# Gate and up projections of a gated MLP as seven block products instead of eight, down products one chunk behind

## The chip, the cores and the metric

One core of a Trainium2 chip runs the whole program. The metric is the device time of one execution in microseconds (us). The engines work in parallel, each through its own list of instructions in order: TensorE (PE in the profile) multiplies matrices, VectorE (DVE) and ScalarE (ACT) do elementwise work, GpSimd (POOL) does elementwise work too and issues some transfers, and SyncE (SP) issues the transfers of the weights. They wait for each other by semaphores.

## The reference

One inference step of a two-layer encoder on 640 token rows (512 of a prompt, 8 sequences of 16). What the change touches is the gated MLP that ends each layer:

```python
def conv_ffn(h, prev, w_gate, w_up, conv_w, conv_b, w_down):
    t = h.shape[1]
    g = h @ w_gate                                   # (tokens, 1024) @ (1024, 2816)
    gp = jnp.concatenate([prev.astype(g.dtype), g], axis=1)
    c = conv_b
    for j in range(CONV_W):                          # 3 taps over time
        c = c + conv_w[j] * gp[:, j:j + t]
    y = (jax.nn.gelu(c) * (h @ w_up)) @ w_down       # (tokens, 2816) @ (2816, 1024)
    return y, gp[:, t:]
...
    h = rmsnorm(x, p["ln_ffn"][l])
    f, tail = conv_ffn(h, conv_prev[l], ...)
    x = x + f
```

All is float32. The other parts of a layer (a mixer, cross-attention, their projections) are the same in both kernels.

## The kernel before

**Products in three parts.** Every float32 operand of the large products is split into a high part, rounded to the type TensorE takes, and a low part, the rest. One product of tiles is three matmuls into the same PSUM bank: weight-low by x-high, weight-high by x-low, high by high (`three`, L792, and the six matmuls of `cols_tile`, L858 to L863). For weights, ACT writes the high part (`w_hi`, L1563) and DVE the low part (`w_lo<-raw,w_hi`, L2093), in units of 128x1024 elements.

**Gate and up.** The 2816 features are 22 tiles of 128 (FT). A chunk ("gu", l, j) holds the weights of tiles 2j and 2j+1 of gate and up: 1024 rows by 512 columns, 4 units, so 11 chunks in each of 2 layers. Features lie on the partitions of the result and the 640 tokens along the free side. A bank holds 512 columns, so `cols_tile` runs each of the 4 outputs (gate and up, 2 tiles each) over 8 row blocks of the input in two pieces of 384 and 256 tokens: 8 x 3 x 2 matmuls, 192 in a chunk. ACT copies the gate out of PSUM to `gp`, applies the first tap (L1912), DVE the other two (L2520, L2521), ACT the gelu (L1919), DVE multiplies with the up result straight out of PSUM (L2524 to L2528), and ACT and DVE split the product `af` in `a_hi` (L1924) and `a_lo` (L2532).

**Down.** ("dn", l, g) multiplies a group of 4 tiles (the first group has 2) with the down weights, for 5 token tiles and 2 column halves, and DVE adds each bank to the residual stream `x` (L2146). Its place is after the chunks of the following group.

**Order and buffers.** Each engine's program is written out by hand as a list and runs in order. Weights are loaded by SP in pieces of two units to `raw`, which has 2 buffers; a load waits until the low parts of the load two places earlier are made. High and low parts lie in 5 slots (W_SLOTS). A slot is filled again when the matmuls of its unit are done. Results of large products rotate over 5 banks (`lin`): the product that takes a bank waits until the result five places earlier has been read out. POOL's part is small: after each squaring of a tile of `x` by ACT it makes the factor of the norm (`norm_rstd`, L538, L539), DVE then scales the tile (`xn<-x,rstd,gain`, L2115), TensorE transposes it (L820), ACT and DVE split the result in `hT_hi` and `hT_lo` (L1624, L2132). In the last projection before the MLP, ("co", l, 1), the norm of a tile runs beside the projection of the next, and the first gate and up products run beside the norm of the last two tiles (`norm_behind`).

## Time and profile before

| | us |
|---|---|
| median of 3 runs (lowest, highest) | 2069.16 (2069.08, 2069.41) |
| the profiled execution | 2069.33 |
| its span, first to last instruction | 2067.5 |
| TensorE busy | 2038.8 (99%) |
| VectorE busy | 981.7 (47%) |
| ScalarE busy | 763.9 (37%) |
| GpSimd busy | 198.6 (10%) |
| granted TensorE clock, mean | 0.997 |

A matmul's recorded duration holds a fixed latency beside its streaming, and consecutive matmuls overlap. What a matmul costs is the distance between its start and the next one's. DVE instructions overlap too, by less than 0.1 us.

The first MLP runs from about 603 us to 1070 us of the span, the second in the last part of the program.

### The profile page before, as it was taken

What the parts mean: (1) busy time and instruction counts of PE and PEld (TensorE: products, weight loads), DVE (VectorE), ACT (ScalarE), POOL (GpSimd) and SP (SyncE); (2) the same over time, 40 slices, a digit from 0 to 9 for tenths busy, and PEclk for the clock granted to TensorE, in tenths of its full rate; (3) what the DMA queues carried; (4) which work ended last, traced back from release to release, by engine and by line L of the source; (5) the groups of instructions that cost most, each with busy time, mean ns of one, the idle gap of its engine ahead of it and who ended that gap; (6) DMA issues with size and microseconds to landing.
All of it is one profiled execution on the core that took longest, in us unless ns stands there. A gap on an engine that the chain in (4) does not pass through costs nothing.

```text
span 2067.5 us, 30583 instructions
## 1 busy us (share of the span) xinstructions
PE 2038.8 (99%) x12398; PEld 1797.0 (87%) x12398; DVE 981.7 (47%) x1648; ACT 763.9 (37%) x1318; POOL 198.6 (10%) x458
## 2 busy tenths in 40 slices
PE   9999989999999999999999999999999999999997
PEld 7889767987789999999989888799778999999996
DVE  5453664435444443443453467653545444343443
ACT  4222552435344233232244447243534433223232
POOL 3012121000100000000010124210010000000001
PEclk9999999999999999999999999999999999999999
DMA  5324143245622122222221211723572222212221
GB/s 176 124 79 149 52 162 129 92 152 187 243 85 83 62 82 83 91 69 62 76 77 62 82 55 34 275 77 117 197 285 85 65 79 82 78 56 82 82 82 55
DMA packets 111066, 219.42 MB, mean 106 GB/s; under 512 B 7011, under 2 KB 52367, under 8 KB 110862
## 3 DMA queue, kind: packets, MB, share of 16 engines
q1 hardware_dynamic: 91234, 148.00, 21.4%
q0 software_dynamic: 19696, 69.47, 9.9%
q8 instruction: 102, 1.67, 0.3%
q14 instruction: 34, 0.28, 0.0%
HBM read 200.51 MB, written 18.24 MB: 106 GB/s over the span
## 4 chain that ended last, share of the span: by engine, by line
PE 95%; DVE 2%; ACT 2%; issue 1%; DMA 0%; POOL 0%; SPq 0%; DVEq 0%; ACTq 0%; POOLq 0%
PE bank L794 15%; PE bank L796 15%; PE bank L795 15%; PE bank L858 7%; PE bank L860 7%; PE bank L862 7%; PE bank L859 5%; PE bank L861 5%; PE bank L863 5%; PE bank L820 1%; PE bank L1240 1%; PE bank L1256 1%; PE bank L1197 1%; PE bank L1282 1%; PE bank L1293 1%
## 5 line engine op out<-in xcount | busy, mean ns | idle before, releaser
L2093 DVE TENSOR_TENSOR w_lo<-raw,w_hi 128x1024 fp32r<-128x1024 f32 x265 | 319.2, 1220 | 508.9 <-ACT w_hi L1563 505.0
L1563 ACT ACTIVATE w_hi<-raw 128x1024 fp32r<-128x1024 f32 x265 | 275.1, 1054 | 254.6 <-PE bank L796 203.5
L794 PE MATMUL bank<-w_hi,hT_lo 128*128 128x512 f32 x720 | 290.7, 404 | 3.1 <-DVE w_lo L2093 1.9
L858 PE MATMUL bank<-hT_hi,w_lo 128*128 128x384 f32 (+1 forms) x856 | 290.1, 339 | 0.0
L860 PE MATMUL bank<-hT_lo,w_hi 128*128 128x384 f32 (+1 forms) x856 | 289.3, 338 | 0.0
L862 PE MATMUL bank<-hT_hi,w_hi 128*128 128x384 f32 (+1 forms) x856 | 289.3, 338 | 0.0
L796 PE MATMUL bank<-w_hi,hT_hi 128*128 128x512 f32 x720 | 281.9, 391 | 0.0
L795 PE MATMUL bank<-w_lo,hT_hi 128*128 128x512 f32 x720 | 281.2, 391 | 0.0
L859 PE MATMUL bank<-hT_hi,w_lo 128*128 128x256 f32 (+1 forms) x856 | 239.0, 279 | 0.0
L861 PE MATMUL bank<-hT_lo,w_hi 128*128 128x256 f32 (+1 forms) x856 | 239.0, 279 | 0.0
L863 PE MATMUL bank<-hT_hi,w_hi 128*128 128x256 f32 (+1 forms) x856 | 239.0, 279 | 0.0
L2146 DVE TENSOR_TENSOR x<-x,bank 128x512 f32<-128x512 f32 x160 | 109.7, 686 | 155.1 <-PE bank L796 154.3
L794 PEld LDWEIGHTS bank<-w_hi,hT_lo 128*128 128x128 f32 x720 | 135.7, 188 | 42.6 <-issue 10.3
L794 PE MATMUL bank<-w_hi,a_lo 128*128 128x512 f32 x440 | 171.7, 390 | 0.0
L796 PE MATMUL bank<-w_hi,a_hi 128*128 128x512 f32 x440 | 171.3, 389 | 0.0
L795 PE MATMUL bank<-w_lo,a_hi 128*128 128x512 f32 x440 | 171.2, 389 | 0.0
L858 PEld LDWEIGHTS bank<-hT_hi,w_lo 128*128 128x128 f32 (+1 forms) x856 | 160.0, 187 | 1.5
L796 PEld LDWEIGHTS bank<-w_hi,hT_hi 128*128 128x128 f32 x720 | 135.5, 188 | 29.5
L859 PEld LDWEIGHTS bank<-hT_hi,w_lo 128*128 128x128 f32 (+1 forms) x856 | 160.1, 187 | 0.5
L862 PEld LDWEIGHTS bank<-hT_hi,w_hi 128*128 128x128 f32 (+1 forms) x856 | 160.0, 187 | 0.6
L860 PEld LDWEIGHTS bank<-hT_lo,w_hi 128*128 128x128 f32 (+1 forms) x856 | 160.0, 187 | 0.6
L861 PEld LDWEIGHTS bank<-hT_lo,w_hi 128*128 128x128 f32 (+1 forms) x856 | 160.1, 187 | 0.2
(372 smaller groups left out, 2997.4 us busy)
## 6 DMA issues: line engine op xcount, KB each, us to landing
raw<-w_ffn_gate SPq DMA_DIRECT2D x44, 512.0 KB, 4.1
raw<-w_ffn_up SPq DMA_DIRECT2D x44, 512.0 KB, 5.1
raw<-w_ffn_down SPq DMA_DIRECT2D x22, 1024.0 KB, 4.9
kcX<-cache_mem_k POOLq DMA_DIRECT2D x16, 1024.0 KB, 6.1
vcX<-cache_mem_v POOLq DMA_DIRECT2D x16, 1024.0 KB, 6.9
raw<-w_in_even SPq DMA_DIRECT2D x13, 1024.0 KB, 5.6
raw<-w_in_odd SPq DMA_DIRECT2D x12, 1024.0 KB, 5.2
raw<-w_cq SPq DMA_DIRECT2D x8, 1024.0 KB, 7.5
```

What stands on the lines that cost most here:

```text
L794: pe.matmul(out, wl, xh, start=first, stop=False)
L795: pe.matmul(out, wh, xl, start=False, stop=False)
L796: return pe.matmul(out, wh, xh, start=False, stop=last)
L858: pe.matmul(oa, wl, hT_hi[:, k, 0:HA], start=f, stop=False)
L859: pe.matmul(ob, wl, hT_hi[:, k, HA:TOK], start=f, stop=False)
L860: pe.matmul(oa, wh, hT_lo[:, k, 0:HA], start=False, stop=False)
L861: pe.matmul(ob, wh, hT_lo[:, k, HA:TOK], start=False, stop=False)
L862: ia = pe.matmul(oa, wh, hT_hi[:, k, 0:HA], start=False, stop=l)
L863: ib = pe.matmul(ob, wh, hT_hi[:, k, HA:TOK], start=False, stop=l)
L1563: act.activation(w_hi[:, g % W_SLOTS, 0:n], raw[:, q % 2, UNIT * i:UNIT * i + n], ACT.Copy).then_inc(*hi_made.mark(c, u))
L2093: dve.tensor_tensor(w_lo[:, s, 0:n], raw[:, q % 2, UNIT * i:UNIT * i + n], flat(w_hi[:, s, 0:n]), ALU.subtract).then_inc(*lo_made.mark(c, u))
L2146: ins = dve.tensor_tensor(xs, xs, lin.bank(c, t, *key)[:, :], ALU.add)
```

## The change

Gate and up become one product of 2x2 blocks: the 640 tokens are cut in two halves of 320, the 1024 input rows in two halves of 512, and the two feature tiles of a chunk are the two column blocks. A form of Strassen's identity makes the four result blocks with seven block products instead of eight. The weights of the products are the blocks A11, A12, A22 and the sums S1 to S4; their partners are the quarters of the transposed input or sums of them (t1, t2, t3, n4).

- The sums of the weights are made in each chunk by POOL, four of 128x1024 (`weight_sum`): S1 = A21+A22 to a buffer of its own, S3 = A11-A21, S2 = S1-A11, S4 = A12-S2 in place in `raw`. A gate-and-up chunk so has 7 units to split by ACT and DVE instead of 4.
- The sums of the input are made once for each layer, by DVE (t1, t2, each in two pieces) and POOL (t3, n4), from `hF`, a copy that ACT makes of the transposed input, and split by ACT and DVE.
- Each of the 7 units is multiplied for gate and for up: 4 row blocks x 3 matmuls of 320 tokens into one bank. A chunk has 14 such products, 168 matmuls.
- The result blocks are put together: ACT copies the first product to `p1` and the second to its place; POOL adds them (`first_corner`); DVE makes u2 = p1 + (S2 product), p1 = u2 + (S1 product), and from these the other three blocks (`to_sums`, `c22`, `c12`, `c21`). The up result is so in SBUF (`af`) when DVE multiplies it with the gelu (`gated`).
- The order of the MLP is a new list, FFN_PLAN: chunks 0 and 1, down group 0, then two chunks and a down group each, at the end chunks 8, 9, 10 and down groups 4 and 5. The taps of the second tile, the gelu, the multiplication and the splits of a chunk are issued among the instructions of the next chunk or down group.
- The first product of the first chunk follows the last projection tile directly; the transposes of the last two norm tiles stand behind the first and third product.

```diff
+FFN_PLAN = [("gu", 0), ("gu", 1), ("dn", 0)]
+for _g in range(1, GROUPS - 2):
+    FFN_PLAN += [("gu", 2 * _g), ("gu", 2 * _g + 1), ("dn", _g)]
+FFN_PLAN += [("gu", FT // 2 - 3), ("gu", FT // 2 - 2), ("gu", FT // 2 - 1), ("dn", GROUPS - 2), ("dn", GROUPS - 1)]
+PARTS = ("A11", "A12", "S1", "S2", "S3", "S4", "A22")
...
@@ sync: loads of the weights @@
-                    sp.wait_ge(*lo_made.at(oc, ou + on - 1))
+                    sp.wait_ge(*lo_made.at(oc, PARTS.index("A22" if ou else "S4") if oc[0] == "gu" else ou + on - 1))
...
@@ gpsimd @@
+                def weight_sum(j, part):
...
+                    pool.tensor_tensor(out, a, b, op).then_inc(*pool_done.mark("sum", l, j, part))
+                def first_corner(j, key):
+                    pool.wait_ge(*lin_a.at(("gu", l, j), (key, "A12")))
+                    dst = gp[0][:, HALO:HALO + HT] if key == "g" else af[0][:, 0:HT]
+                    pool.tensor_tensor(dst, dst, p1[key][:, :], ALU.add)...
...
@@ tensor @@
+                def gate_up(j, between={}):
+                    for u, part in enumerate(PARTS):
+                        wait_unit(c, u)
+                        if j == 0:
+                            wait_operand(part)
+                        hi, lo = operand[part]
+                        for m, key in enumerate("gu"):
+                            out = lin.open(pe, c, (key, part))
+                            for k in range(KT // 2):
+                                cols = slice(P * (2 * k + m), P * (2 * k + m) + P)
+                                ins = three(out[:, 0:HT], weight(c, u, False)[:, cols], weight(c, u, True)[:, cols], lo[:, k, :], hi[:, k, :],
+                                            k == 0, k == KT // 2 - 1)
+                            ins.then_inc(*lin_full.mark(c, (key, part)))
+                            if (part, key) in between:
+                                between[part, key]()
...
-                            cols_tile(c, f"ffn{l}", P * e, ("g", e))
-                            cols_tile(c, f"ffn{l}", 256 + P * e, ("u", e), last=e == 1)
+                        gate_up(i, {("A11", "g"): lambda: norm_tile(nm, T - 2), ("A12", "g"): lambda: norm_tile(nm, T - 1)} if i == 0 else {})
...
@@ vector @@
+                def to_sums(j, key):
+                    dve.wait_ge(*pool_done.at("C11", l, j, key))
+                    dve.wait_ge(*lin_full.at(c, (key, "S2")))
+                    dve.tensor_tensor(u2[key][:, :], p1[key][:, :], lin.bank(c, (key, "S2"))[:, 0:HT], ALU.add)...
+                    dve.tensor_tensor(p1[key][:, :], u2[key][:, :], lin.bank(c, (key, "S1"))[:, 0:HT], ALU.add)...
...
+                sum_t(0)
+                low_ts(0)
+                sum_t(1)
+                low_ts(1)
+                halves(nm, T - 1)
```

**The GpSimd list at the start of the MLP.** L538 and L539 (L592 and L593 in the new file) are the two instructions of a norm tile; `sum`, `sumN` and `raw` written by L763 are the weight sums. Before:

```order
L538 TENSOR_SCALAR rstd<-sq_sum 128x1
L539 TENSOR_TENSOR rstd<-rstd,half_neg 128x1
L538 TENSOR_SCALAR rstd<-sq_sum 128x1
L539 TENSOR_TENSOR rstd<-rstd,half_neg 128x1
L696 COPY gp_184<-prevT 128x8x2
L698 COPY tailc<-gp_184 128x2
```

and now:

```order
L592 TENSOR_SCALAR rstd<-sq_sum 128x1
L593 TENSOR_TENSOR rstd<-rstd,half_neg 128x1
L763 TENSOR_TENSOR raw<-sum_199,raw 128x8x128
L592 TENSOR_SCALAR rstd<-sq_sum 128x1
L593 TENSOR_TENSOR rstd<-rstd,half_neg 128x1
L763 TENSOR_TENSOR raw<-raw 128x8x128
L796 TENSOR_TENSOR t3F<-hF 128x1280
L798 TENSOR_TENSOR hF<-hF,t2F 128x4x320
L771 COPY gp_201<-prevT 128x8x2
L771 COPY gp_202<-prevT 128x8x2
L777 TENSOR_TENSOR gp_201<-gp_201,p1g 128x320
L777 TENSOR_TENSOR af_205<-af_205,p1u 128x320
```

A weight sum now follows directly on each norm tile from the second on, and two sums of the input follow the last.

**The VectorE list at the start of the first chunk.** `hF`, `t2F` and `t_lo` are the sums of the input. Before:

```order
L2093 TENSOR_TENSOR w_lo<-raw,w_hi 128x1024 x3
L2146 TENSOR_TENSOR x<-x,bank 128x512
L2115 SCALAR_TENSOR_TENSOR xn<-x,rstd,gain 128x1024
L2132 TENSOR_TENSOR hT_lo<-bank,hT_hi 128x4x128 x4
L2093 TENSOR_TENSOR w_lo<-raw,w_hi 128x1024
```

and now:

```order
L2409 TENSOR_TENSOR x<-x,bank 128x512
L2369 SCALAR_TENSOR_TENSOR xn<-x,rstd,gain 128x1024
L2389 TENSOR_TENSOR hT_lo<-bank,hT_hi 128x4x128
L2785 TENSOR_TENSOR hF<-hF 128x4x192
L2787 TENSOR_TENSOR t2F<-hF 128x4x192
L2791 TENSOR_TENSOR hT_lo<-hF,hT_hi 128x4x192
L2791 TENSOR_TENSOR t_lo<-t2F,t_hi 128x4x192
L2785 TENSOR_TENSOR hF<-hF 128x4x128
L2787 TENSOR_TENSOR t2F<-hF 128x4x128
L2791 TENSOR_TENSOR hT_lo<-hF,hT_hi 128x4x128
L2791 TENSOR_TENSOR t_lo<-t2F,t_hi 128x4x128
```

Eight instructions on the sums of the input stand behind the scaling of the last norm tile, before anything of the chunk.

**The VectorE list between two chunks.** From the last instruction on the banks of a chunk to the first on those of the next. Before, such an instruction stands in every tile (L2524 to L2528):

```order
L2093 TENSOR_TENSOR w_lo<-raw,w_hi 128x1024 x3
L2520 SCALAR_TENSOR_TENSOR cv_187<-gp_185,conv_par,cv_187 128x656
L2521 SCALAR_TENSOR_TENSOR cv_187<-gp_185,conv_par,cv_187 128x656
L2524 TENSOR_TENSOR af_189<-cv_187,bank 128x384
L2526 TENSOR_TENSOR af_189<-cv_187,bank 128x128
```

and now:

```order
L2840 TENSOR_TENSOR af_206<-u2u,bank 128x320
L2849 SCALAR_TENSOR_TENSOR cv_204<-gp_202,conv_par,cv_204 128x656
L2850 SCALAR_TENSOR_TENSOR cv_204<-gp_202,conv_par,cv_204 128x656
L2861 TENSOR_TENSOR af_205<-cv_203,af_205 128x512
L2864 TENSOR_TENSOR af_205<-cv_203,af_205 128x128
L2339 TENSOR_TENSOR w_lo<-raw,w_hi 128x1024
L2869 TENSOR_TENSOR a_lo<-af_205,a_hi 128x640
L2861 TENSOR_TENSOR af_206<-cv_204,af_206 128x512
L2864 TENSOR_TENSOR af_206<-cv_204,af_206 128x128
L2339 TENSOR_TENSOR w_lo<-raw,w_hi 128x1024
L2869 TENSOR_TENSOR a_lo<-af_206,a_hi 128x640
L2339 TENSOR_TENSOR w_lo<-raw,w_hi 128x1024
```

Eleven instructions with all their tensors in SBUF stand in a row, and the next bank is read only behind them.

## Rows read from the trace of the kernel before

**Rows 1.** The page: busy time, and the chain that ended last by engine.

```profile
PE 2038.8 (99%) x12398; PEld 1797.0 (87%) x12398; DVE 981.7 (47%) x1648; ACT 763.9 (37%) x1318; POOL 198.6 (10%) x458
...
PE 95%; DVE 2%; ACT 2%; issue 1%; DMA 0%; POOL 0%; SPq 0%; DVEq 0%; ACTq 0%; POOLq 0%
```

**Rows 2.** Waits of TensorE: us in total, times, longest.

```profile
PE bank L1016 <- DVE sA L2348: 3.2, 3, 2.4
...
PE bank L794 <- DVE hT_lo L2132: 0.7, 3, 0.3
```

**Rows 3.** Timeline of PE: start us, duration us, instruction, at the first MLP.

```profile
611.65 0.33 PE L794 MATMUL bank<-hT_hi,w_lo 128*128 128x384 f32 x1
...
613.56 0.33 PE L796 MATMUL bank<-hT_hi,w_hi 128*128 128x384 f32 x1
613.73 0.28 PE L794 MATMUL bank<-hT_hi,w_lo 128*128 128x256 f32 x1
...
619.36 0.28 PE L796 MATMUL bank<-hT_hi,w_hi 128*128 128x256 f32 x1
619.48 0.34 PE L858 MATMUL bank<-hT_hi,w_lo 128*128 128x384 f32 x1
...
626.52 0.34 PE L858 MATMUL bank<-hT_hi,w_lo 128*128 128x384 f32 x1
```

**Rows 4.** Groups of DVE by shape, whole run: count | busy us, mean ns.

```profile
L2093 DVE TENSOR_TENSOR w_lo<-raw,w_hi 128x1024 fp32r<-128x1024 f32 x264 | 318.9, 1224 | 504.8 <-ACT w_hi L1563 500.8
...
L2521 DVE SCALAR_TENSOR_TENSOR cv<-gp,conv_par,cv 128x656 f32<-128x656 f32 x44 | 39.7, 902 | 1.6
...
L2532 DVE TENSOR_TENSOR a_lo<-af,a_hi 128x640 fp32r<-128x640 f32 x44 | 36.3, 826 | 35.5 <-ACT a_hi L1924 35.5
L2524 DVE TENSOR_TENSOR af<-cv,bank 128x384 f32<-128x384 f32 x44 | 24.4, 555 | 44.7 <-PE bank L862 25.8 <-ACT cv L1919 18.9
```

**Rows 5.** Group of ACT by shape, whole run.

```profile
L1563 ACT ACTIVATE w_hi<-raw 128x1024 fp32r<-128x1024 f32 x264 | 274.8, 1057 | 254.6 <-PE bank L796 203.5 <-PE bank L863 42.3 <-DMA raw<-w_in_even 4.9
```

**Rows 6.** Timeline of POOL and DVE, two stretches where both work.

```profile
1242.94 3.24 DVE L2569 SCALAR_TENSOR_TENSOR of<-of,hs_rstd,gnorm 128x256 f32<-128x256 f32 x2 [0.81 <-POOL hs_rstd L717]
...
1243.61 0.41 POOL L729 TENSOR_TENSOR xL<-bcum 128x128 f32<-128x128 f32 x1
...
1245.79 0.89 POOL L735 TENSOR_TENSOR aI<-bcum 128x256 f32<-128x256 f32 x1
...
1274.79 1.11 POOL L753 TENSOR_TENSOR aS<-bcum 128x512 f32<-128x512 f32 x1
1274.93 2.43 DVE L2569 SCALAR_TENSOR_TENSOR of<-of,hs_rstd,gnorm 128x256 f32<-128x256 f32 x2 [0.81 <-POOL hs_rstd L717]
...
1275.84 1.24 POOL L755 TENSOR_TENSOR kdS<-bcum 128x512 f32<-128x512 f32 x1
```

**Rows 7.** DVE L2569 and L2588, 256 elements each: duration ns min/median/max.

```profile
L2569 DVE SCALAR_TENSOR_TENSOR of<-of,hs_rstd,gnorm x20: 477/546/2679, 1207.3 to 1320.3; 128x256 f32<-128x256 f32 x20
...
L2588 DVE SCALAR_TENSOR_TENSOR qI<-qI,cqT x8: 411/421/422, 1180.5 to 1269.7; 128x256 f32<-128x256 f32 x8
```

**Rows 8.** Timeline at the start of the first MLP, all engines.

```profile
608.04 0.55 POOL L539 TENSOR_TENSOR rstd<-rstd,half_neg 128x1 f32<-128x1 f32 x1
...
608.69 1.29 DVE L2115 SCALAR_TENSOR_TENSOR xn<-x,rstd,gain 128x1024 f32<-128x1024 f32 x1 [2.20 <-POOL rstd L539]
...
610.03 1.25 PE L820 MATMUL bank<-ident,xn 128*128 128x128 f32 x8
```

**Rows 9.** The clock: TensorE's timeline after its longest wait, and windows with PEclk.

```profile
269.12 0.66 PE L1016 MATMUL bank<-ident,sA 128*128 128x128 f32 x4 [2.35 <-DVE sA L2348]
...
270.00:275.00 5.00, 5.00 (x23) 4.20 (x23) 2.44 (x6) 1.55 (x3) 1.44 (x2) 0.66 0.99 360
```

**Rows 10.** The page: weight loads, KB each, median us from issue to landing.

```profile
raw<-w_ffn_gate SPq DMA_DIRECT2D x44, 512.0 KB, 4.1
raw<-w_ffn_up SPq DMA_DIRECT2D x44, 512.0 KB, 5.1
```

More of the change, by code:

```diff
@@ L123, in rest @@
         out += [("co", l, 0), ("co", l, 1)]
-        for g in range(GROUPS):
-            out += [("gu", l, j) for j in group_pairs(g)]
-            if g:
-                out.append(("dn", l, g - 1))
-        return out + [("dn", l, GROUPS - 1)]
+        return out + [(kind, l, i) for kind, i in FFN_PLAN]
     chunks += rest(0)
@@ L156 @@
 for _c in CHUNKS:
-    for _u in range(0, units_of(_c), 2):
-        _n = min(2, units_of(_c) - _u)
+    for _u in range(0, raw_units(_c), 2):
+        _n = min(2, raw_units(_c) - _u)
         for _i in range(_n):
@@ new lines, in rest @@
+                pool.wait_ge(*dve_done.at("t2F", l, 1))
+                pool.tensor_tensor(hF[:, 1, :, 0:HT], hF[:, 1, :, 0:HT], t2F[:, :, :], ALU.subtract).then_inc(*pool_done.mark("n4F", l))
+                pool.wait_ge(*act_done.at("prevT", l))
+                for j in range(FT // 2):
+                    more = j + 1 < FT // 2
+                    halo(2 * j)
+                    halo(2 * j + 1)
+                    first_corner(j, "g")
+                    first_corner(j, "u")
+                    if more:
+                        weight_sum(j + 1, "S1")
+                        weight_sum(j + 1, "S3")
+                    tails(2 * j)
+                    if more:
+                        weight_sum(j + 1, "S2")
+                    tails(2 * j + 1)
+                    if more:
+                        weight_sum(j + 1, "S4")
@@ L1309, in rest @@
                     ins.then_inc(*aux_full.mark("prevT", l, n))
[L1310 to L1311 removed]
+                nm = f"ffn{l}"
+                for t in range(T):
+                    if t:
+                        proj_out(("co", l, 1), t)
+                    else:
+                        out_steps(("co", l, 1), 0, 2, 8)
+                    if 0 < t < T - 1:
+                        norm_tile(nm, t - 1)
@@ L2472, in rest @@
                 add_x(("co", l, 0), TP, 0)
-                out_half(1, ("co", l, 1), f"cross{l}", f"ffn{l}")
+                nm = f"ffn{l}"
+                for t in range(T):
+                    if t == 1:
+                        split_lo(NEXT[("co", l, 1)], [0])
+                    if t == T - 1:
+                        split_lo(NEXT[("co", l, 1)], [1, 2, 3])
+                    add_x(("co", l, 1), t, 1, f"cross{l}")
+                    scaled(nm, t)
+                    if t:
+                        halves(nm, t - 1)
                 def down(g):
@@ L2535, in rest, with sum_t @@
-                down(GROUPS - 1)
+                def sum_t(n):
+                    for half in range(2):
+                        dve.wait_ge(*act_done.at("hF", l, T - 1 if n else T - 2, half))
+                    w, v = CUT[n], slice(HT + CUT[n].start, HT + CUT[n].stop)
+                    dve.tensor_tensor(hF[:, 0, :, w], hF[:, 0, :, v], hF[:, 0, :, w], ALU.subtract).then_inc(*dve_done.mark("t1F", l, n))
+                    dve.wait_ge(*dve_done.at("t1F", l, n))
+                    dve.tensor_tensor(t2F[:, :, w], hF[:, 1, :, v], hF[:, 0, :, w], ALU.subtract).then_inc(*dve_done.mark("t2F", l, n))
@@ new lines, in c21 @@
+                def c21(j, key):
+                    c = ("gu", l, j)
+                    dve.wait_ge(*lin_full.at(c, (key, "A22")))
+                    dve.wait_ge(*lin_v.at(c, (key, "S3")))
+                    dst = gp[1][:, HALO:HALO + HT] if key == "g" else af[1][:, 0:HT]
+                    dve.tensor_tensor(dst, u2[key][:, :], lin.bank(c, (key, "A22"))[:, 0:HT], ALU.add).then_inc(*lin_v.mark(c, (key, "A22")))
+                    if key == "g":
+                        dve_done.after("gate", l, 2 * j + 1)
```

443 lines of the change are left out of this document (348 added, 95 removed).

## The prediction

> **What bounds the kernel now.** I read the page first: TensorE is busy 99% of the span, the chain that ended last runs 95% through it, and no other engine is above 47% [rows 1]. Then TensorE's waits: its largest one was 2.4 us in a piece of attention, and on the norm's operands ahead of projections it waited 0.7 us in all [rows 2]. So the program is a row of matmuls, and in the MLPs it has no gap. What a matmul costs there I read from the distance of starts in its timeline [rows 3]: 12 matmuls of 384 columns begin from 611.65 to 613.56 us, 1.91/11 = 0.1736 us each; 48 of 256 columns from 613.73 to 619.36 us, 5.63/47 = 0.1198 us each; and one tile of `cols_tile`, 24 pairs, takes 626.52 - 619.48 = 7.04 us, 0.2933 us a pair, which is the sum of the two. Last I read the groups of VectorE and the stretches where GpSimd and VectorE both work, since the change loads these two.
>
> **What TensorE gains.** Removed are 22 chunks x 96 pairs = 2112 pairs: 2112 x 0.2933 = 619.5 us. Added are 22 x 168 = 3696 matmuls of 320 columns. The trace has none, but it has both neighbours; halfway between 0.1198 and 0.1736 is 0.1467 us, so 542.2 us. The ends are 0.1198 x 3696 = 443 us and 0.1736 x 3696 = 642 us; I take the midpoint, since the two rows lie on one line with the 7.04 us tile. Down products, transposes and the rest keep their number. The gain is 77.3 us. A product of 12 matmuls lasts 1.76 us, a weight unit 3.52 us, a chunk 24.64 us instead of 28.16 us.
>
> **What VectorE and GpSimd get.** For each chunk VectorE has 7 low parts, which start 1.15 us apart in a queue (1.22 us recorded, ends overlap) [rows 4]: 8.1 us. Reading out banks is twelve 320-column operations; between 0.42 us for 256 elements [rows 7] and 0.56 us for 384 [rows 4], less the overlap of 0.08 us, 0.40 us each: 4.9 us. Four taps of 0.9 us are 3.6 us, two multiplications of 640 elements 1.6 us, two low parts of `a` 1.5 us [rows 4]. Sum about 20 us in 24.64 us; before it was far below half. ScalarE gets three more high parts of 1.06 us [rows 5] and the copies, about 14 us, and is not the limit. GpSimd gets four sums of 1024 elements: 128 elements take 0.41 us and 512 take 1.11 us [rows 6], 1.8 ns an element, so 2.05 us each, and two `first_corner` of 0.76 us: 9.8 us.
>
> **The two do not run side by side.** In the stretch at 1242.9 us two VectorE instructions of 256 elements took 3.24 us together, the second 2.68 us, while GpSimd's row of subtractions ran; at 1274.9 us two took 2.43 us, each ending only after a GpSimd subtraction of 512 elements [rows 6]. Undisturbed such an instruction takes 0.42 us [rows 7]. All operands of these lie in SBUF. So a VectorE instruction with two SBUF inputs waits out a GpSimd instruction that reads SBUF, and GpSimd waits too (L735 took 0.89 us). I see no such stretch of a VectorE instruction that reads a bank. The Trainium skill, "SBUF — State Buffer", section "Who interferes with whom", says this as a rule against the change: the two share a read interface, and whoever issues first keeps it for the whole instruction. The trace agrees (2.68 us for 0.42 us of work).
> Of VectorE's 20 us in a chunk 14.8 us have two SBUF inputs (low parts, taps, multiplications), and GpSimd's 9.8 us all read SBUF. In a pair of chunks between two down groups the sums for the second chunk fall in the first one; those for the chunk after fall in the down group, where VectorE has room.
>
> **Start of an MLP.** Here the sum goes along the row of instructions. Before, the factor of the last norm tile ends at 608.6 us, VectorE scales at 608.69 us for 1.29 us, TensorE transposes at 610.03 us [rows 8]. Now a weight sum follows each factor on GpSimd without a wait, so it has the port when VectorE's scaling (two SBUF inputs) comes 0.1 us later: 2.05 us later for each of four tiles. VectorE has little room between these tiles, so it adds up: by my timeline the transposes of the third tile come 1.0 us late, the first block product 1.6 us, the transposes of the last tile 3.7 us (block products of 7 us stand ahead of S1, and only three of the four can hide it). Behind the last tile come copy, t1, t2, their splits back and forth between ScalarE and VectorE in two pieces, about 6.6 us from the scaled tile to the operand of S1, with 2.7 us of TensorE work left beside it: 3.9 us. Together 10.2 us. If GpSimd's t3 (1280 elements, 2.5 us) takes the port ahead of the second piece, 12.7 us. Without any blocking only the last chain is left, and one late tile: 4.4 us. I take 10.5 us a layer, ends 4.4 and 12.7.
>
> **Between chunks.** A product may take its bank when the one five places earlier has been read. The S1 product for gate waits for S2 (full 12.5 us after the chunk's start), VectorE reads both in 1 us, and the bank is wanted at 15.84 us: 2.3 us of room. In the first chunk of a pair nothing is left over from before, and VectorE keeps up until the loads land (issue after the low part of S4, then some 5 us [rows 10]). Then S1, S3, S2, S4 of the next chunk, 2.05 us each, stand one by one ahead of a low part or a tap. By my timeline VectorE is through with the first chunk's banks at 29.5 us, with taps, multiplications and splits at 41.4 us, and with the S2 and S1 products at 42.3 us, where the bank was wanted at 40.5 us: TensorE waits 1.9 us in the second chunk. Without blocking VectorE is there by 35 us, and the wait is nothing. The second chunk makes no sums, so the next pair starts clean. Chunks 8, 9, 10 have no down group between them: 1.9 us and then 5.6 us. Chunk 0 begins late and is followed by chunk 1: 4 us. So 3 x 1.9 + 1.9 + 5.6 + 4 = 17.2 us a layer at most by this reckoning, 0 at least. Small errors in 40 us of reckoning move it by as much as the wait itself, and a wait of TensorE gives VectorE time back; I take 12 us.
>
> **The clock.** After 2.35 us without work (266.8 to 269.1 us) the granted clock was at the lower level, 1.2 GHz, for a part of the next 5 us, mean 0.66 [rows 9]: 5 x 0.34 = 1.7 us lost. The waits at the start of an MLP are that long. One such loss a layer, 1.7 us, ends 0 and 3.4.
>
> **The sum.** The profiled execution took 2069.33 us (span 2067.5), 0.2 us above the median of 2069.16. 2069.3 - 77.3 + 2 x (10.5 + 12 + 1.7) = 2040.4 us.
> What I cost at nothing: down products one chunk behind and the later splits of `a`: they are done some 8 us into the next chunk or down group, and the down group that needs them begins at least 24 us after. Without that cover TensorE would wait those 8 us at each group.
>
> **Rivals.**
> 1. Nothing blocks between chunks and little at the start; TensorE stays the bound. For it: VectorE has 4.6 us free in each chunk by plain sums. Against: rows 6. 2069.3 - 77.3 + 2 x 4.4 = 2001 us, up to 2015 us with a few waits.
> 2. The blocking is as in my timeline at full: 2 x (12.7 + 17.2 + 1.7) = 63.2 us: 2055 us. Against: a wait of TensorE makes the next one smaller.
> 3. Slower: the weight sums read and write `raw` in rows of 128 in place, and GpSimd takes 2.6 us or more for each instead of 2.05 us. Four of them are on VectorE's path, so each wait of 1.9 us becomes 4 us, passes the 2.35 us after which the clock fell, and costs 1.7 us more. A layer then loses 12.7 + 4 x 5.7 + 10 + 6 + 1.7 = 53 us, both 106 us: 2069.3 - 77.3 + 106 = 2098 us. It decides where a layer's waits pass 77.3/2 = 38.6 us, at about 2.35 us for a sum. For it: L735 and L755 already took 0.89 and 1.24 us when disturbed.
> 4. The change doesn't do what it says: 320 columns cost as 384 do. 642 instead of 542 us: 2140 us. Against: rows 3 show cost in proportion to columns.
>
> **How the numbers follow.** Forecast 0.44, own range 2022 to 2050 us; rival 1 0.22; rival 2 0.18; rival 3 0.13; rival 4 0.03. The measurement can tell about 0.2% (4 us) from no change. Faster: forecast, rivals 1 and 2 but for their upper ends, 0.81; within 0.2% 0.05, out of rivals 2 and 3; slower 0.14. The range from 2003 to 2072 us leaves out half of rival 1's lower end, most of rival 3 and rival 4.
>
> **What would show it.** TensorE: 320-column matmuls 0.147 us apart, in the busy row; VectorE about 20 us of work in a chunk, but recorded durations of `w_lo`, taps and `xn` with a long tail (2 to 3.4 us maximum) where GpSimd's sums run; `xn` in the MLP's norm about 2 us longer; TensorE's waits on VectorE's S1 operand (4 us, twice) and on banks read by `to_sums` of chunks 1, 3, 5, 7, 9, 10; the granted clock low once or twice at each MLP's start. If the longest `w_lo` is 1.23 us, the blocking is wrong and rival 1 holds; if a sum takes over 2.4 us, rival 3.

## The result and the profile after

The kernel became slower: 2106.74 us (median of 4 runs, 2105.28 to 2108.38) against 2069.12 us for the kernel before beside it; ratio 1.0184, 95% interval 1.0167 to 1.0202. The forecast was 2040, the range ended at 2072. The changed kernel's profiled span is 2103.5 us. The page, busy time and the chain by engine, answers to [rows 1]:

```profile
PE 1992.7 (95%) x11870; PEld 1731.5 (82%) x11870; DVE 1334.4 (63%) x1994; ACT 834.0 (40%) x1368; POOL 548.6 (26%) x594
...
PE 66%; DVE 21%; issue 4%; DMA 4%; ACT 3%; POOL 1%; SPq 0%; DVEq 0%; ACTq 0%; POOLq 0%
```

TensorE has less to do, but the chain that ended last runs through it for 66% instead of 95%, and 21% of it is VectorE. TensorE's timeline shows the new matmuls, 51 of 320 columns from the first of these rows to the second, answering to [rows 3]:

```profile
735.74 0.31 PE L909 MATMUL bank<-hT_hi,w_lo 128*128 128x320 f32 x1
...
743.09 0.31 PE L911 MATMUL bank<-t_hi,w_hi 128*128 128x320 f32 x1
744.83 0.42 PE L909 MATMUL bank<-t_hi,w_lo 128*128 128x320 f32 x1 [1.43 <-DVE p1g L2805]
```

7.35/50 = 0.147 us each, as forecast. The products' gain is there. It is lost in waits, which answer to [rows 2] (us in total, times, longest):

```profile
PE bank L909 <- DVE x L2409: 25.2, 8, 11.6
PE bank L909 <- DVE p1g L2805: 17.1, 12, 1.4
PE bank L909 <- DVE hT_lo L2791: 8.5, 2, 4.2
PE bank L935 <- DVE xn L2369: 8.1, 4, 3.5
PE bank L909 <- DVE gp L2840: 7.2, 4, 2.1
PE bank L909 <- DVE w_lo L2343: 6.1, 8, 1.1
```

All six are waits for VectorE. Its groups (count | busy, mean ns) answer to [rows 4]: what cost 1224, 902 and 826 ns now costs far more in the MLPs, and the first line, low parts outside the block products, does not.

```profile
L2343 DVE TENSOR_TENSOR w_lo<-raw,w_hi 128x1024 fp32r<-128x1024 f32 x177 | 212.7, 1217 | 210.5 <-ACT w_hi L1724 207.0
L2339 DVE TENSOR_TENSOR w_lo<-raw,w_hi 128x1024 fp32r<-128x1024 f32 x132 | 197.5, 1501 | 52.2 <-ACT w_hi L1721 51.7
L2849 DVE SCALAR_TENSOR_TENSOR cv<-gp,conv_par,cv 128x656 f32<-128x656 f32 x44 | 91.6, 2081 | 0.0
...
L2339 DVE TENSOR_TENSOR w_lo<-sumN,w_hi 128x1024 fp32r<-128x1024 f32 x20 | 45.4, 2269 | 0.0
L2869 DVE TENSOR_TENSOR a_lo<-af,a_hi 128x640 fp32r<-128x640 f32 x40 | 45.2, 1130 | 6.4 <-ACT a_hi L2112 6.4
```

GpSimd's weight sums, one line of the kernel by operands (ns min/median/max):

```profile
L763 POOL TENSOR_TENSOR raw<-raw x44: 2338/3152/3406, 592.2 to 2012.9; 128x1024 f32<-128x1024 f32 x44
L763 POOL TENSOR_TENSOR sumN<-raw x20: 2385/2410/2555, 639.0 to 2000.2; 128x1024 f32<-128x1024 f32 x20
L763 POOL TENSOR_TENSOR raw<-sumN,raw x20: 2384/2405/3002, 646.0 to 2007.2; 128x1024 f32<-128x1024 f32 x20
```

A sum alone takes 2.40 us, not 2.05, and the 88 of them take 2.70 us each in the mean, since GpSimd is held too. The start of the first MLP, VectorE's and GpSimd's timeline, answers to [rows 8]: the last tile's scaling takes 3.29 us instead of 1.29, with a sum that began 0.14 us ahead of it, and the t1 of the second piece 3.41 us for an operation of 0.7.

```profile
609.55 0.55 POOL L593 TENSOR_TENSOR rstd<-rstd,half_neg 128x1 f32<-128x1 f32 x1
610.07 2.34 POOL L763 TENSOR_TENSOR raw<-raw 128x1024 f32<-128x1024 f32 x1
617.88 2.88 POOL L796 TENSOR_TENSOR t3F<-hF 128x1280 f32<-128x1280 f32 x1 [5.46 <-ACT hF L1797]
```
```profile
610.21 3.29 DVE L2369 SCALAR_TENSOR_TENSOR xn<-x,rstd,gain 128x1024 f32<-128x1024 f32 x1 [2.20 <-POOL rstd L593]
...
617.90 3.41 DVE L2785 TENSOR_TENSOR hF<-hF 128x512 f32<-128x512 f32 x1
```

The largest wait is in down group 0. The group has two tiles, so a product is 6 matmuls or 1.36 us, and five banks are full after 6.8 us. VectorE's timeline there:

```profile
679.89 0.47 DVE L2840 TENSOR_TENSOR af<-u2u,bank 128x320 f32<-128x320 f32 x1
680.29 2.61 DVE L2849 SCALAR_TENSOR_TENSOR cv<-gp,conv_par,cv 128x656 f32<-128x656 f32 x1
682.93 0.90 DVE L2850 SCALAR_TENSOR_TENSOR cv<-gp,conv_par,cv 128x656 f32<-128x656 f32 x1
683.75 2.83 DVE L2861 TENSOR_TENSOR af<-cv,af 128x512 f32<-128x512 f32 x1
...
687.85 2.96 DVE L2869 TENSOR_TENSOR a_lo<-af,a_hi 128x640 fp32r<-128x640 f32 x1
...
693.15 3.57 DVE L2409 TENSOR_TENSOR x<-x,bank 128x512 f32<-128x512 f32 x5
```
```profile
693.89 0.79 PE L909 MATMUL bank<-w_hi,a_lo 128*128 128x512 f32 x1 [11.64 <-DVE x L2409]
```

The first read of a bank of the group stands behind 13 us of taps, multiplications and low parts, three of them held by sums, which makes up about 6 of the 13 us (the taps operation of 2.61 us stands beside one of 0.90). ScalarE's high parts take as long as in [rows 5] and the loads, once issued, as long as in [rows 10], so neither has become slower. When a load can be issued is another matter (e8):

```profile
L1721 ACT ACTIVATE w_hi<-raw 128x1024 fp32r<-128x1024 f32 x132 | 138.5, 1055 | 276.2 <-PE bank L911 131.6 <-DMA raw<-w_ffn_up 100.9 <-POOL raw L763 43.7
```
```profile
raw<-w_ffn_gate SPq DMA_DIRECT2D x44, 512.0 KB, 4.0
raw<-w_ffn_up SPq DMA_DIRECT2D x44, 512.0 KB, 5.1
```

Last the clock, windows of both places (us; PE busy, PEld, DVE, ACT, POOL busy; granted clock, DMA share, GB/s), answering to [rows 9]. The lower level, 1.2 GHz, was granted in stretches of 13.7 us from 612.7, 684.4 and 1691.3, in two of 6.8 us from 1619.7 and 1629.9, and in two of 3.4 us. One of 8.0 us at the very end of the program has nothing to do with the change: the kernel before has one of 7.2 us there.

```profile
612.00:627.00 15.00, 9.21 (x37) 8.84 (x38) 14.78 (x12) 8.22 (x13) 8.18 (x7) 0.54 0.00 1
684.00:699.00 15.00, 5.11 (x14) 4.06 (x15) 12.53 (x14) 2.10 (x3) 7.46 (x6) 0.54 0.00 0
```

### The profile page after: what moved, and what is told of

The parts are those of the page before. It is cut to its first block, busy times and chain, and to the rows that moved or that the text cites. A ratio compares the mean times of both kernels' runs of the same rounds, so it can differ in the third digit from the quotient of the medians.

```text
span 2103.5 us, 30087 instructions
## 1 busy us (share of the span) xinstructions
PE 1992.7 (95%) x11870; PEld 1731.5 (82%) x11870; DVE 1334.4 (63%) x1994; ACT 834.0 (40%) x1368; POOL 548.6 (26%) x594
## 4 chain that ended last, share of the span: by engine, by line
PE 66%; DVE 21%; issue 4%; DMA 4%; ACT 3%; POOL 1%; SPq 0%; DVEq 0%; ACTq 0%; POOLq 0%
PE bank L909 16%; PE bank L911 15%; PE bank L910 15%; DVE w_lo L2339 6%; DVE cv L2849 4%; DMA raw<-w_ffn_down 2%; DMA raw<-w_ffn_up 2%; PE bank L973 2%; PE bank L975 2%; PE bank L977 2%; DVE w_lo L2343 1%; DVE af L2861 1%; PE bank L1355 1%; PE bank L1371 1%; DVE xn L2369 1%
## 5 line engine op out<-in xcount | busy, mean ns | idle before, releaser
L2343 DVE TENSOR_TENSOR w_lo<-raw,w_hi 128x1024 fp32r<-128x1024 f32 x177 | 212.7, 1217 | 210.5 <-ACT w_hi L1724 207.0
L909 PE MATMUL bank<-hT_hi,w_lo 128*128 128x320 f32 (+2 forms) x800 | 254.5, 318 | 21.7 <-DVE hT_lo L2791 8.5
L911 PE MATMUL bank<-hT_hi,w_hi 128*128 128x320 f32 (+2 forms) x800 | 251.6, 314 | 0.0
L910 PE MATMUL bank<-hT_lo,w_hi 128*128 128x320 f32 (+2 forms) x800 | 251.5, 314 | 0.0
L2339 DVE TENSOR_TENSOR w_lo<-raw,w_hi 128x1024 fp32r<-128x1024 f32 x132 | 197.5, 1501 | 52.2 <-ACT w_hi L1721 51.7
L909 PEld LDWEIGHTS bank<-hT_hi,w_lo 128*128 128x128 f32 x800 | 154.6, 193 | 27.3 <-issue 12.4
L910 PEld LDWEIGHTS bank<-w_lo,hT_hi 128*128 128x128 f32 x720 | 135.5, 188 | 25.3
L910 PEld LDWEIGHTS bank<-hT_lo,w_hi 128*128 128x128 f32 x800 | 154.5, 193 | 0.4
L911 PEld LDWEIGHTS bank<-hT_hi,w_hi 128*128 128x128 f32 x800 | 154.3, 193 | 0.0
L763 POOL TENSOR_TENSOR raw<-raw 128x1024 f32<-128x1024 f32 x44 | 130.3, 2961 | 73.5 <-DVE w_lo L2339 73.5
L909 PE MATMUL bank<-t_hi,w_lo 128*128 128x320 f32 x352 | 111.3, 316 | 21.8 <-DVE p1g L2805 17.1
```

The source lines that it names most:

```text
L763: pool.tensor_tensor(out, a, b, op).then_inc(*pool_done.mark("sum", l, j, part))
L909: pe.matmul(out, wl, xh, start=first, stop=False)
L910: pe.matmul(out, wh, xl, start=False, stop=False)
L911: return pe.matmul(out, wh, xh, start=False, stop=last)
L2339: dve.tensor_tensor(lo, part_source(c, u), flat(hi), ALU.subtract).then_inc(*lo_made.mark(c, u))
L2343: dve.tensor_tensor(w_lo[:, s, 0:n], raw[:, q % 2, UNIT * i:UNIT * i + n], flat(w_hi[:, s, 0:n]), ALU.subtract).then_inc(*lo_made.mark(c, u))
```

## The experiments

Two theories for the lost time. **A, an order:** VectorE does the right work, but what TensorE waits for stands late in its queue. **B, the price of the sums:** each sum on GpSimd takes 2.40 us and holds VectorE's operations with two inputs in SBUF. All kernels ran against the kernel before (2066.9 to 2068.6 us beside them); each is the changed kernel (2106.7 us) with one edit unless said. To place the differences I took from each trace the distance from the first matmul of one chunk to the first of another, mean of the two layers. Without any wait chunk 0 with its 16 transposes would take 26.4 us, chunk 1 and group 0 24.6 + 13.6 = 38.3 us, and chunks 2 to 10 with three groups 303.4 us.

| kernel | time, us | chunk 0 | chunk 1 and group 0 | chunks 2 to 10 |
|---|---|---|---|---|
| changed kernel | 2106.7 | 39.2 | 59.7 | 323.8 |
| e1_dn0 | 2093.6 | 38.6 | 53.3 | 324.1 |
| e2_small | 2025.8 | 35.6 | 47.2 | 303.0 |
| e3_start | 2101.0 | 38.3 | 60.0 | 325.0 |
| e4_warm | 2106.3 | 38.7 | 59.7 | 323.8 |
| e5_dvesum | 2059.0 | 35.0 | 55.0 | 311.7 |
| e6_all | 2070.1 | 31.8 | 49.0 | 325.4 |
| e7_split | 2096.1 | 37.6 | 56.8 | 325.2 |
| e8_order | 2142.0 | 39.4 | 59.5 | 339.9 |
| e9_chain | 2043.6 | 33.0 | 47.4 | 313.3 |
| e10_best | 2037.3 | 33.0 | 42.9 | 315.3 |
| e11_floor | 2011.0 | 32.5 | 42.9 | 303.1 |
| e12_orders | 2086.5 | 35.8 | 52.4 | 324.4 |

**e1_dn0: group 0's banks read between the other work.**

```diff
-gated(f); refill_lo(g0 + 4); low_a(f); gated(f + 1); low_a(f + 1); down(0)
+add_x(0,0); gated(f); add_x(0,1); low_a(f); add_x(1,0); gated(f + 1)
+add_x(1,1); refill_lo(g0 + 4); add_x(2,0); low_a(f + 1); the other five
```

> VectorE takes the first five banks of down group 0 between its other work (one bank after the taps, one after each of: first gated product, low part, second gated product, S1 refill) instead of after all of it. Nothing is added or left out. Theory A (an order: the group is two tiles long, its five banks are full after 6.8 us, and VectorE has some 13 us of other work queued ahead of the first of its ten reads): the waits of 11.64 us at 693.89 and 11.65 at 1700.92 fall to under 2 us each, the half-clock stretches of 13.7 us at 684.4 and 1691.3 go with them (about 2.1 us each), and the kernel takes 2107 - 2 x 12 = 2083 us, between 2078 and 2088. Rival B (the price of the sums: VectorE has too much to do between the second chunk and the third, whatever the order): the same 11 us turn up as waits before or in chunk 2, and the time stays within 2100 to 2107.

Measured 2093.62 us (2093.38 to 2094.76), ratio 1.0126 (1.0111 to 1.0141). 13 us, half of what theory A gave. TensorE's waits for `x` (whole run: total, times, longest) show why:

```profile
PE bank L909 <- DVE x L2409: 9.8, 11, 2.3
```

In place of the wait of 11.6 us stand three of up to 2.3 us: with the order mended VectorE is still late, which is theory B's part.

**e2_small: the sums' price taken away.**

```diff
-pool.tensor_tensor(out, a, b, op)
+pool.tensor_tensor(out[:, 0:1, 0:16], a[:, 0:1, 0:16], b[:, 0:1, 0:16], op)
```

> GpSimd's weight sums cover 16 of their 1024 columns (the output is wrong by what is left out; the two sum tiles are cleared once per layer), everything else is as in the changed kernel. It takes away the 2.4 us that each sum holds VectorE's two-input operations. Theory B (blocking is what costs): the operations of 2.5 to 3.4 us on VectorE fall to their undisturbed 0.7 to 1.2 us, the waits at the transposes (3.50) and at the first S1 product (4.24) fall to about 1.4 and 2, that in down group 0 from 11.6 to about 4, those of 2.0 in the second chunk and the eleventh go, and the kernel takes 2107 - 2 x (2.1 + 2.2 + 7.6 + 3) - about 8 of clock = 2069 us, between 2060 and 2076. Theory A (order alone): VectorE's queue still stands ahead of group 0's reads; at most 10 us in all are saved, 2097 or above.

Measured 2025.75 us (2023.46 to 2026.45), ratio 0.9793 (0.9777 to 0.981). 81 us less than the changed kernel, twice what theory B had said: the expectation gave chunks 2 to 10 at most 3 us a layer, and 20.8 went there. The groups of VectorE are as in [rows 4] again (a taps operation 896 ns instead of 2081, a low part from `sumN` 1219 instead of 2269):

```profile
L2852 DVE SCALAR_TENSOR_TENSOR cv<-gp,conv_par,cv 128x656 f32<-128x656 f32 x44 | 39.4, 896 | 0.0
...
L2342 DVE TENSOR_TENSOR w_lo<-sumN,w_hi 128x1024 fp32r<-128x1024 f32 x20 | 24.4, 1219 | 1.5 <-ACT w_hi L1724 1.5
```

and from chunk 2 to chunk 10 TensorE loses nothing: 303.0 us. Two long waits per layer are left:

```profile
PE bank L912 <- DVE hT_lo L2794: 13.1, 2, 6.6
PE bank L912 <- DVE x L2412: 11.3, 2, 5.6
```

The edit takes away two things at once, the holds of VectorE and the time that a sum itself needs before ScalarE and VectorE can split its result. So the 81 us are the price of both together.

**e3_start: GpSimd's sums kept off the scalings.**

```diff
 norm_rstd(ffn, [t])
+pool.wait_ge(*xn_made.at(ffn, t))     # t = 1, 2, 3, each ahead of its sum
 weight_sum(0, ...)
-norm_rstd(ffn, [T - 1]); weight_sum(0, "S4")
+weight_sum(0, "S4"); norm_rstd(ffn, [T - 1])
+pool.wait_ge(*dve_done.at("t1", l, 1))  # ahead of t3
```

> Only at the start of each MLP: GpSimd begins each sum of the first chunk after VectorE has scaled the tile whose factor it has just made, makes S2 and S4 ahead of the last tile's factor, and begins the difference t3 after VectorE has made the second low part of t1. If the waits of 3.50 and 4.24 us there come from operations of VectorE that GpSimd's held (3.3 us instead of 1.2, 3.4 instead of 0.7), they fall to about 1.4 and 1.5, the wait of 1.1 goes, and with them at least half of the half-clock stretch of 13.7 us: 2 x (5.9 + 3) = 18 us less, 2089, between 2084 and 2095. Rival (TensorE waits there for a chain of transposes, copies and subtractions that is long by itself, as it must with the last tile's factor late): under 6 us saved, 2101 or more.

Measured 2100.97 us (2097.26 to 2103.88), ratio 1.0159 (1.0144 to 1.0175): 5.8 us, so the expectation missed; 2101 is what its rival said, a chain that is long by itself. The mean scaling did fall from 1783 to 1284 ns:

```profile
L2373 DVE SCALAR_TENSOR_TENSOR xn<-x,rstd,gain 128x1024 f32<-128x1024 f32 x33 | 42.4, 1284 | 46.0 <-POOL rstd L593 45.7
```

but the S4 sum (3.33 us from 604.09) now held a low part for 3.43 us from 605.06, which stands ahead of the last addition to `x`; the last factor came at 611.2 us instead of 610.1, and the wait ahead of the last transposes stayed (3.93 us). The wait of 1.1 us at the first block product went, and the one at S1 fell from 4.24 to 2.56 us. I had moved a hold, not removed it. The rival isn't refuted either: of the 39.2 - 26.4 = 12.8 us that chunk 0 loses, 9.2 are still there with cut sums (e2).

**e4_warm: the clock held up.** TensorE is given 26, 32 and 90 matmuls on old data in front of the three long waits of a layer.

```diff
+for _ in range(n): pe.matmul(bank[:, 0:256], hT_hi[:, 0, 0:P], hT_hi[:, 0, 0:256])
```

> TensorE is given matmuls of 256 columns on old data, into a bank that the next real product overwrites, at three waits of each MLP: 26 ahead of the last tile's transposes, 32 ahead of the first S1 product, 90 in down group 0 ahead of its sixth product. The waits themselves stay. If the half-clock stretches (13.7 us at 612.7 and 684.4, 6.8 + 6.8 at 1619.7, 13.7 at 1691.3) come from TensorE's idle time, they go and give back their cost, the busy time in them at half speed: 4.3 + 2.1 in the first layer, 5.6 + 2.1 in the second, 14 us, so 2093, between 2089 and 2098. Rival: the waits alone explain the loss and the clock gives nothing back, 2105 or more (or the fill runs past the end of a wait and costs a little).

Measured 2106.28 us (2103.36 to 2110.0), ratio 1.0187 (1.0172 to 1.0202). The clock did rise, in the same windows as above:

```profile
612.00:627.00 15.00, 11.87 (x80) 11.49 (x79) 14.78 (x12) 7.88 (x12) 8.18 (x6) 0.89 0.01 2
684.00:699.00 15.00, 13.97 (x101) 13.08 (x101) 13.99 (x15) 2.23 (x3) 8.53 (x7) 1.00 0.00 0
```

and the time did not move. At these places TensorE at full speed only waits longer for VectorE; in this kernel the half-clock stretches are a mark of the loss, not a part of it.

**e5_dvesum: the sums on VectorE.** In a chunk followed by another:

```diff
 c12(i, "g")
+weight_sum(i + 1, "S1")       # dve.tensor_tensor, was pool
 c12(i, "u")
+weight_sum(i + 1, "S3")
 refill_lo(g0 + 9)
+weight_sum(i + 1, "S2")       # S4 behind the taps that come next
```

> All 88 weight sums move from GpSimd to VectorE (same operands; each some 1.2 us there, as the low part of a unit with as many elements): in a chunk followed by another beside the differences of its last products, in one followed by a down group between that group's additions, for the first chunk between the additions and scalings of the last four tiles. Theory B (what costs is that each sum on GpSimd holds VectorE for up to its 2.4 us): VectorE gets 88 x 1.2 = 106 us more of its own work, and loses the 133 us by which its busy time (1334 us) stood above what cut sums left of it (1201); it is busy some 1307 us and late less often. 2107 - 81 (cut sums) + 5 to 25 for what the sums now delay: 2031 to 2051, most likely 2040. Rival A (VectorE has simply too much to do per chunk; taking in the sums makes it worse): 2107 or more.

Measured 2058.99 us (2057.78 to 2059.99), ratio 0.9958 (0.9944 to 0.9972). Already faster than the kernel before, 48 us faster than the changed one, but 8 us past the top of the expectation. VectorE's busy time fell from 1334.4 to 1302.8 us though it took over 88 sums: they take 1.22 us each, less than GpSimd's had cost it in holds.

```profile
L2723 DVE TENSOR_TENSOR raw<-raw 128x1024 f32<-128x1024 f32 x44 | 53.7, 1220 | 0.6
```

**e6_all: everything together.** e5's sums, e1's order, e8's order (below), and at the start:

```diff
-sum_t(0); low_ts(0); sum_t(1); low_ts(1)
+sum_t(0); low t1 0; sum_t(1); low t1 1; low t2 0; low t2 1
+dve.tensor_tensor(t3F, ...)          # t3 and n4 were on GpSimd
```

> The sums on VectorE; group 0's first five banks read between its other work; each first sum of products ahead of the refill that stood before it; at the start the first block sum's operand made ahead of the second's, and the differences t3 and n4 on VectorE too. Theory B with A for the rest: the two waits that cut sums left in each layer (6.55 us at the first S1 product, 5.65 in down group 0) fall to about 2.5 and 1, 2 x 8.7 = 17 us, and the sums on VectorE cost 5 to 20: 2026 - 17 + 5 to 20 = 2014 to 2029, most likely 2020, faster than the kernel before. If the orders count for nothing beside VectorE's load, it equals the sums on VectorE alone, 2040.

Measured 2070.08 us (2067.42 to 2074.42), ratio 1.0017 (1.0008 to 1.0027): worse than e5, and outside both theories. The table shows where: chunk 0 (31.8) and group 0 (49.0) gained as meant, chunks 2 to 10 lost 13.7 us a layer.

**e7_split: each sum in four pieces.**

```diff
-pool.tensor_tensor(out, a, b, op)
+for v in range(4): pool.tensor_tensor(out[:, 2*v:2*v+2], a[:, 2*v:2*v+2], b[:, 2*v:2*v+2], op)
```

> Each weight sum on GpSimd is made in four pieces of 256 columns instead of one of 1024; the work is the same. If an operation of VectorE with two inputs in SBUF waits until the operation of GpSimd that is under way ends, and GpSimd's next one waits for VectorE's in turn, such an operation now loses at most some 0.6 us instead of 2.4, while the pieces wait for VectorE three times more per sum: VectorE's longest low parts fall from 3.0 to under 2 us, the sums end later, and the time falls by 15 to 35 us, 2072 to 2092. Rival (the two engines share one port by the element, so only the number of elements counts): nothing changes within 5 us, 2102 to 2112.

Measured 2096.12 us (2092.91 to 2096.43), ratio 1.0137 (1.0122 to 1.0152). 10.6 us, below the expectation, though its mechanism is there: VectorE's busy time fell by 87 us, to 1246.9, since a hold is as long as the piece. The longest low part of a unit of the block products fell from 3.44 to 1.90 us. But the pieces wait in turn, and there are four times as many (median 742 ns, up to 1744), so that a sum takes 3.92 us in the mean instead of 2.70:

```profile
L765 POOL TENSOR_TENSOR raw<-raw x176: 714/742/1734, 593.1 to 2005.9; 128x256 f32<-128x256 f32 x176
```
```profile
L2342 DVE TENSOR_TENSOR w_lo<-raw,w_hi x132: 1209/1374/1899, 582.8 to 2014.0; 128x1024 fp32r<-128x1024 f32 x132
```

VectorE's idle time ahead of the low parts of the same loop, for ScalarE's high parts, rose from 51.7 to 99.2 us: the sums came later.

```profile
L2342 DVE TENSOR_TENSOR w_lo<-raw,w_hi 128x1024 fp32r<-128x1024 f32 x132 | 187.6, 1422 | 99.5 <-ACT w_hi L1724 99.2
```

In the chain that ended last VectorE's share fell from 21% to 12% and GpSimd's rose from 1% to 7%:

```profile
PE 66%; DVE 12%; POOL 7%; DMA 6%; issue 5%; ACT 4%; SPq 0%; DVEq 0%; POOLq 0%; ACTq 0%
```

So what TensorE waits for depends on how long a sum takes as well as on how long it holds VectorE, and no run parts the two: e7 shortens the holds and lengthens the sums, e2 and e5 shorten both.

That fits the page of the Trainium skill named in the prediction ("SBUF — State Buffer", "Who interferes with whom"): the hold lasts a whole instruction, as the page has it for VectorE's two-port modes. The trace shows the same for operations with two inputs, at most 1.90 us beside pieces of 0.74 where it was 3.44 beside sums of 2.40. Shorter instructions share it out, they do not remove it.

**e8_order: the first sum of products ahead of a refill.**

```diff
-refill_lo(g0 + 6)
 to_sums(i, "g")
+refill_lo(g0 + 6)
 to_sums(i, "u")
```

> One change of order on VectorE in chunks 1 to 10: the first pair of sums of products (for gate) stands ahead of the refill of the last unit instead of behind it. Twelve waits of TensorE in the profile are of 1.43 us and end with that sum. If they are the order's alone they go, 12 x 1.6 = 19 us, 2088. If VectorE is simply behind there (it is what sets the pace, and fills of TensorE's waits with other work gave nothing), the refill behind it is late instead and little is won: 2100 to 2107.

Measured 2141.98 us (2138.58 to 2143.76), ratio 1.036 (1.0345 to 1.0376): 35 us slower, which neither side of the expectation had. The twelve waits of 1.43 us for `p1g` went, and these came (the changed kernel had 7.2 and 6.1 us on the last two lines):

```profile
PE bank L909 <- DVE x L2409: 24.1, 8, 11.7
PE bank L909 <- DVE gp L2840: 22.0, 12, 2.1
PE bank L909 <- DVE w_lo L2343: 19.4, 9, 2.5
```

The sum waits for the S2 product, and the refill now waits behind it. That refill is the last reader of a half of `raw`, whose next load is issued after it; GpSimd's idle time ahead of the first sum, until that load came, rose from 225.2 to 252.2 us:

```profile
L763 POOL TENSOR_TENSOR sumN<-raw 128x1024 f32<-128x1024 f32 x20 | 48.1, 2404 | 271.9 <-DMA raw<-w_ffn_up 252.2 <-issue 19.8
```

The wait of 1.43 us was the cheaper of the two. In e6 the same edit cost 26.5 us (e9 below).

**e9_chain: e6 without that edit.**

```diff
-to_sums(i, "g"); refill_lo(g0 + 6); to_sums(i, "u")
+refill_lo(g0 + 6); to_sums(i, "g"); to_sums(i, "u")
```

> As the version with everything together, but each first sum of products stands behind the refill again, as in the changed kernel: sums on VectorE, group 0's banks read between other work, the first block sum's operand made ahead of the second's. Moving that sum ahead of the refill cost 35 us by itself; in the version with everything the waits of 2.1 to 2.3 us at each down group and of 3.2 in the last chunk are the same ones. If that order was all that spoiled it, they go, and what is left of the gains stands: 2059 (sums on VectorE) - 2 x 3.7 (start) - 2 x 5.6 (group 0) = 2040, between 2034 and 2046. Rival: the orders at the start and in group 0 only move VectorE's lateness to later places, 2055 to 2062.

Measured 2043.57 us (2041.37 to 2045.34), ratio 0.9881 (0.9865 to 0.9898), as expected. Moving orders does win time once VectorE is no longer held.

**e10_best: group 0 once more.**

```diff
-refill_lo(g0 + 10)                    # at the end of chunk 1, waits for a load
 c21(i, "u")
+add_x(0,0); taps(f + 1); gated(f); add_x(0,1)
+refill_lo(of chunk 1, g0 + 10)        # ScalarE's high part moved likewise
```

> As the last, and in group 0 of each layer the refill of chunk 2's second unit, which waits for a load, no longer stands ahead of the sum that frees the last bank of chunk 1: it is made behind group 0's second addition, the first addition comes right behind that sum, and the last four refills and sums lie between the others. The wait of about 2 us ahead of the fifth product and those of 1.7 and 1.2 behind it go: 2 x 4.5 = 9 us less than the last kernel, 2031, between 2026 and 2037. Rival (the load itself sets the time at which chunk 2 can begin): within 2 us of the last kernel.

Measured 2037.3 us (2035.45 to 2038.91), ratio 0.9852 (0.9838 to 0.9867). 6 us less than e9, short of the 9 expected: chunk 1 and group 0 fell from 47.4 to 42.9 us a layer, and chunks 2 to 10 gave 2 back. This is the best version with the whole computation: 30 us faster than the kernel before, 3 us from the forecast, by another way than the forecast's.

**e11_floor: cut sums and mended orders.** e9 with this in place of the sums on VectorE:

```diff
-dve.tensor_tensor(out, a, b, op)
+pool.tensor_tensor(out[:, 0:1, 0:16], a[:, 0:1, 0:16], b[:, 0:1, 0:16], op)
```

> Sums cut to 16 of 1024 columns on GpSimd (the output is wrong by that), group 0's banks read between other work, and the first block sum's operand first, with the differences t3 and n4 on VectorE: the block form with its sums at nothing and both orders mended. The two waits per layer that cut sums left (6.55 and 5.65 us) fall to about 2.5 and 1: 2026 - 2 x 8.7 = 2009, between 2004 and 2015, which is the forecast's sum (2040.4) less all its waits and clock (2 x 24.2) within the noise of 1992 + start and first-group rests. Rival: they are the chain's own length, 2020 to 2026.

Measured 2011.0 us (2008.61 to 2011.22), ratio 0.9723 (0.9708 to 0.9737), as expected. All that is left above 2069.1 - 77.3 = 1991.8 us are 6.1 and 4.6 us a layer in the first two columns: the forecast's gain of the products is confirmed within 3 us.

**e12_orders: e10's orders with the sums on GpSimd.**

```diff
-dve.tensor_tensor(out, a, b, op)
+pool.tensor_tensor(out, a, b, op)      # at its old places
```

> The orders of the last version that beat the kernel before (start of each MLP, group 0, the moved refill), with the weight sums back on GpSimd: the fourth corner beside the changed kernel (2107), sums on VectorE (2059) and both (2037). If the two repairs are independent, the orders give here the 22 us that they give there: 2085, between 2079 and 2091. If group 0's late reads came from the order alone, as theory A had it, more than twice that is won, 2062 or less. If GpSimd's sums spoil the new orders too (each of VectorE's operations there is held again), less than 12: 2095 or more.

Measured 2086.5 us (2084.9 to 2087.11), ratio 1.0089 (1.0071 to 1.0107), as expected. The four corners, 2106.7, 2059.0, 2086.5 and 2037.3, make the two repairs nearly independent: sums 48 to 49 us, orders 20 to 22 us. Both theories hold in part, and B is the larger.

## Why the prediction was wrong

- **The gain of 77.3 us** was right: 0.147 us a matmul, and e11's time.
- **The blocking** was right as a mechanism. **Its size was not: the sum "so 2.05 us each" is a mis-sized term.** A sum alone takes 2.40 us, and 2.70 in the mean, because I had written that GpSimd waits too and put that at nothing. All 88 with their mutual holds cost 81 us (e2). I had drawn a line through 128 and 512 elements of [rows 6], which are other operations with operands laid out otherwise. The sum's own operation takes 0.74 us for 256 elements (e7) and 2.40 for 1024, 2.2 ns an element and not 1.8. The Trainium skill has a price that bears on this: "GPSIMD Engine Reference", section "Elementwise — side-by-side cycle accounting", gives 4497 ns for a `tensor_tensor` of 2048 elements, by which an estimate for 1024 is 2.25 us; this trace's 2.40 us lies above even that.
- **Between chunks** I took 12 us a layer, 17.2 at most. Measured, chunks 2 to 10 alone lose 323.8 - 303.0 = 20.8 us a layer, where my terms gave them 9.2 (12/17.2 of 13.2). The wait that I had reckoned came where I had it, at `p1g` in chunks 3, 5, 7, 9 and 10, and it was smaller than I had it, 1.43 us each. What I had at nothing are the other waits and the stretches at half clock, about 13 us. TensorE's waits from 703 to 1025.5 us, chunks 2 to 10 of layer 0 (total, times, longest):

```profile
PE bank L909 <- DVE p1g L2805: 7.1, 5, 1.4
PE bank L909 <- DVE w_lo L2343: 2.3, 3, 0.9
PE bank L909 <- DVE gp L2840: 2.0, 1, 2.0
PE bank L909 <- ACT p1u L2080: 1.8, 2, 1.0
```

  The whole loss goes with cut sums, so it was the sums' price, and I had followed it along one path alone.
- **"What I cost at nothing: down products one chunk behind and the later splits of `a`" is the step that failed outright.** I asked whether the splits are done before the group that needs them, and they are. I did not ask what they stand ahead of. Where chunk 1 is followed by group 0, they stand ahead of ten reads of banks that fill in 1.36 us each. The "down group, where VectorE has room" lasts 27 us for four tiles, and 13.6 us for two. Chunk 1 and group 0 lost 21.4 us a layer; of my 12 us their share was 2.8. Of these 21.4, 12.5 go with the sums (e2), and a further 4.3 with the orders (e11).
- **The start**: 10.5 us and 1.7 of clock forecast; 39.2 - 26.4 = 12.8 us measured, the 3.50 and 4.24 us waits at the places named, and one of 1.1 us ahead of the first block product, where I had 1.6. So the number came out and the places too. The shares did not: 3.6 us of the 12.8 go with cut sums (e2), where I had put 6.1 down to blocking, and 9.2 stay. With t1's operands first and t3 and n4 off GpSimd as well 6.1 stay (e11); how much of that gain is the order and how much the hold of 2.7 us by t3, no run parts. That the sum was right is in part luck.
- **The clock**: one loss of 1.7 us a layer was forecast; the matmuls that ran at half pace in the stretches above add 8 to 9 us a layer to TensorE's row, half of the 16 and 19 us that it worked in them. They are within the losses of the three columns, not beside them. By e4 giving them back gains nothing that can be measured, since VectorE sets the pace there. As a term of a sum it was counted where it does not add.
- In sum, forecast 24.2 us a layer, measured 12.8 + 21.4 + 20.8 = 55.0; 2 x 30.8 = 62 of the 66.3 us of error. I did not place the rest for certain. It may lie outside the three columns: against e11 the first block product of layer 0 comes 3.5 us later (603.7 us, 600.2 there), and from the end of chunk 10 to the first block product of layer 1 it takes 3.8 us longer (586.0 us, 582.2 there).
- **Rival 3**, at 0.13, is what happened in sign and in part in cause, with 2.40 us for a sum past its 2.35. Its own ledger was off: waits of 4 us at `to_sums` did not come (1.43 us), and group 0 was not in it. That its 106 us lie near the 110 measured is luck. Without the 18.6 us by which group 0 and chunk 1 went past my share for them a layer would have lost 36.4 us, under the 38.6 that decide the sign. So by this ledger the price of the sums, as far as I had followed it, ends about where the kernel before is, and chunk 1 with group 0, late by sums and order together, turned the sign. Having found that a seventh more on one estimated duration turned the sign, I should have given it far more than 0.13.
- Rival 2's terms at their full, 31.6 us a layer, are passed by 55.0 for the same reasons. Rivals 1 and 4 are out; rival 1's 2001 us is not reached even with sums cut, because of group 0 and the chain at the start.
